# Cross-attention in a one-core decoder step: the samples' values weighed in column quarters of TensorE, all eight samples' values resident

## What is computed

```python
def cross_attend(h, w_xq, w_xo, mem_k, mem_v):
    b, l, _ = h.shape
    q = (h @ w_xq).reshape(b, l, X_HEADS, X_HEAD_DIM)
    s = jnp.einsum('blhd,bmhd->bhlm', q, mem_k).astype(F32) * (X_HEAD_DIM ** -0.5)
    p = jax.nn.softmax(s, axis=-1).astype(mem_v.dtype)
    o = jnp.einsum('bhlm,bmhd->blhd', p, mem_v).reshape(b, l, D_MODEL)
    return o @ w_xo
```

## Time and profile before

| | us |
|---|---|
| median of 3 runs (2934.2 to 2935.93) | 2935.62 |
| the profiled execution's own time | 2925.83 |
| span of the profiled execution | 2924.1 |
| phase `cross`, its first DMA issue to the first matmul of the next phase | 1924.57 to 2044.81 |

### The profile page before, as it was taken

One profiled execution on the slowest core, in us unless ns is written; L12 is line 12 of the kernel. 1 busy time (PEld: TensorE's weight loads), 2 busy tenths in 40 slices (PEclk: granted clock), 3 DMA queues, 4 the chain that ended last, 5 costly groups with the idle time before them and its releaser, 6 DMA issues. The chain is left out here.

```text
span 2924.1 us, 44166 instructions
## 1 busy us (share of the span) xinstructions
PE 2717.6 (93%) x15387; PEld 2195.3 (75%) x15387; DVE 1838.5 (63%) x2530; ACT 803.8 (27%) x1460; POOL 352.3 (12%) x581
## 2 busy tenths in 40 slices
PE   6789899999999999988879789988989999999998
PEld 4457666666666667865525789973989999999998
DVE  6559999899898937867552462564264444444445
ACT  4231211211111213049712541331051111111115
POOL 1010032322322211200122000031000000000000
PEclk7789999999999999999979799998999999999999
DMA  9876699989999835521197431144111111111111
GB/s 354 298 258 202 190 336 320 341 296 315 330 317 317 310 98 176 165 63 30 58 289 250 153 122 36 37 146 160 55 42 46 43 50 43 50 43 43 43 57 60
DMA packets 334116, 478.19 MB, mean 164 GB/s; under 512 B 26600, under 2 KB 215397, under 8 KB 332110
## 3 DMA queue, kind: packets, MB, share of 16 engines
q1 hardware_dynamic: 291110, 333.29, 34.5%
q0 software_dynamic: 42416, 142.32, 14.2%
q10 hardware_dynamic: 408, 0.31, 0.0%
HBM read 453.22 MB, written 22.62 MB: 163 GB/s over the span
## 5 line engine op out<-in xcount | busy, mean ns | idle before, releaser
L84 ACT ACTIVATE whi<-raw 128x1024 fp32r<-128x1024 f32 (+1 forms) x184 | 189.7, 1044 | 924.3 <-PE banks L113 807.7
L111 PE MATMUL banks<-ffn_hhi,whi 128*128 128x344 f32 x1056 | 339.9, 322 | 8.0 <-DVE ffn_hlo L141 5.1
L112 PE MATMUL banks<-ffn_hlo,whi 128*128 128x344 f32 x1056 | 338.6, 321 | 0.0
L113 PE MATMUL banks<-ffn_hhi,wlo 128*128 128x344 f32 x1056 | 338.6, 321 | 0.0
L111 PE MATMUL banks<-ffn_ghi,whi 128*128 128x344 f32 (+1 forms) x880 | 315.7, 359 | 10.8 <-DVE xT L1771 5.3
L113 PE MATMUL banks<-ffn_ghi,wlo 128*128 128x344 f32 (+1 forms) x880 | 310.8, 353 | 0.0
L112 PE MATMUL banks<-ffn_glo,whi 128*128 128x344 f32 (+1 forms) x880 | 309.8, 352 | 0.0
L88 DVE TENSOR_TENSOR wlo<-raw,whi 128x1024 fp32r<-128x1024 f32 (+1 forms) x184 | 222.5, 1215 | 134.7 <-ACT whi L84 134.4
L111 PE MATMUL banks<-a_hhi,whi 128*128 128x512 f32 x704 | 287.9, 409 | 6.9 <-DVE wlo L88 6.1
L624 DVE TENSOR_TENSOR ffn_kt<-ffn_kt,ffn_q 128x1024 f32<-128x1024 f32 x224 | 272.9, 1219 | 28.2 <-DMA ffn_kt<-in_cache_k_dram 28.2
L611 POOL DMA_DIRECT2D ffn_vt<-in_cache_v_dram x384 | 206.7, 538 | 654.4 <-issue 648.7
(11 more groups left out here) (474 smaller groups left out, 4762.8 us busy)
## 6 DMA issues: line engine op xcount, KB each, us to landing
ffn_kt<-in_cache_k_dram SPq DMA_DIRECT2D x448, 256.0 KB, 4.3
ffn_vt<-in_cache_v_dram POOLq DMA_DIRECT2D x384, 256.0 KB, 5.0
raw<-in_w_ffn_gate_dram SPq DMA_DIRECT2D x44, 512.0 KB, 4.5
raw<-in_w_ffn_up_dram SPq DMA_DIRECT2D x44, 512.0 KB, 4.1
raw<-in_w_ffn_down_dram SPq DMA_DIRECT2D x44, 512.0 KB, 4.6
last_kt<-in_cache_k_dram POOLq DMA_DIRECT2D x64, 256.0 KB, 3.1
s_vt<-in_cache_v_dram POOLq DMA_DIRECT2D x64, 256.0 KB, 5.1
s_vt<-in_cache_v_dram SPq DMA_DIRECT2D x64, 256.0 KB, 4.8
```

What stands on the lines that cost most here:

```text
L84: act.activation(self.k.whi[c % W_RING][:, 0:self.width], self.slots[s][:, 0:self.width], ACT.Copy).then_inc(self.hi_done, 1)
L111: pe.matmul(out, whi, rhi, start=first, stop=False)
L112: pe.matmul(out, whi, rlo, start=False, stop=False)
L113: return pe.matmul(out, wlo, rhi, start=False, stop=last)
```

## The change

In `cross`, the samples' values get eight places of their own: four in the space of `qT`, one in that of `mkT`, one in that of `qb`, and slots 2 and 3 of `cache`. SP loads them in three steps: five once the last scores are out (`sc_ps` at 8), one once the last product is done, two once the last keys are reduced. The next phase's first two weight blocks follow at once. PE takes four samples at a time: the matmul of sample `first + c` writes partitions 32c to 32c+31 of the bank, and the four matmuls of one k and half stand one behind the other. So each quarter of the 128 partitions holds the sum over two samples. `masked`, `mask` and `sel` grow from 32 to 128 partitions; the mask is made a quarter at a time, and POOL starts with its products only after that.

```diff
-        sel = place("c_sel", [32, NS], 44.9)
-        masked = place("c_masked", [32, D], 32.5)
-        mask = place("c_mask", [32, D], 137.5)
+        sel = place("c_sel", [P, NS], 44.9)
+        masked = place("c_masked", [P, D], 32.5)
+        mask = place("c_mask", [P, D], 137.5)
         qb = place("c_qb", [P, 2, D], 129.5)
         cache = place("c_cache", [P, 4, 2, D], 0, ring=True)
+        in_qT = place("c_v_in_q", [P, 4, 2, D], 97)
+        values = [in_qT[:, j] for j in range(4)] + [place("c_v_in_k", [P, 2, D], 48)[:, :, :], place("c_v_in_qb", [P, 2, D], 129.5)[:, :, :],
+                                                    cache[:, 2], cache[:, 3]]
...
                 def load(n):
                     if n >= 4:
-                        if n - 4 < NS:
-                            sp.wait_ge(q["reduced"], n - 3)
-                        else:
-                            sp.wait_ge(q["v_used"], n - 4 - NS + 1)
-                    src = a["cache_mem_k" if n < NS else "cache_mem_v"][n % NS].rearrange("(b p) n -> p b n", p=P)
-                    sp.dma_start(cache[:, n % 4], src).then_inc(cache_in[n % 4], 16)
+                        sp.wait_ge(q["reduced"], n - 3)
+                    sp.dma_start(cache[:, n % 4], a["cache_mem_k"][n].rearrange("(b p) n -> p b n", p=P)).then_inc(cache_in[n % 4], 16)
...
-                for n in range(2 * NS - 4):
-                    if n + 2 < NS:
-                        query(n + 2)
-                    load(n + 4)
+                for n in range(NS - 2):
+                    query(n + 2)
+                    if n + 4 < NS:
+                        load(n + 4)
+                sp.wait_ge(q["sc_ps"], GR)
+                for b in range(5):
+                    load_v(b)
+                sp.wait_ge(q["product"], NS)
+                load_v(5)
+                sp.wait_ge(q["reduced"], NS)
+                load_v(6)
+                load_v(7)
                 for n in range(RAW_RING):
-                    sp.wait_ge(q["v_used"], 5)
                     self.load_ahead(sp, "xo", n)
...
-                v.tensor_tensor(masked[:, :], self.psum[0:32, 1024:2048], mask[:, :], ALU.mult).then_inc(q["kept"], 1)
+                v.tensor_tensor(masked[:, :], self.psum[:, 1024:2048], mask[:, :], ALU.mult).then_inc(q["kept"], 1)
...
                 pe.wait_ge(q["exped"], GR)
-                for b in range(NS):
-                    pe.wait_ge(q["padded"], b + 1)
-                    pe.wait_ge(cache_in[b % 4], 16 * (2 + b // 4 + 1))
+                for first in (0, 4):
+                    pe.wait_ge(q["padded"], first + 4)
+                    for c in range(4):
+                        pe.wait_ge(v_in[first + c], 16)
                     for k in range(2):
                         for half in range(2):
-                            ins = pe.matmul(ps[2 + half][0:32, :], pad[:, b, k], cache[:, b % 4, k, half * 512:(half + 1) * 512],
-                                            start=b == 0 and k == 0, stop=b == NS - 1 and k == 1)
-                    ins.then_inc(q["all_v"] if b == NS - 1 else q["v_used"], 1)
+                            for c in range(4):
+                                b = first + c
+                                ins = pe.matmul(ps[2 + half][32 * c:32 * c + 32, :], pad[:, b, k], values[b][:, k, half * 512:(half + 1) * 512],
+                                                start=first == 0 and k == 0, stop=first == 4 and k == 1)
+                ins.then_inc(q["all_v"], 1)
```

More of the change, by code:

```diff
@@ L2994, in cross @@
         qb_in = [self.sem(f"c_qb_in{r}") for r in range(2)]
+        v_in = [self.sem(f"c_v_in{b}") for b in range(NS)]
         REDUCED_IN = {2: (0,), 3: (1,), 4: (2,), 5: (3, 4), 6: (5,), 7: (6, 7)}
@@ L3000, in load, with load_v @@
                     if n >= 4:
-                        if n - 4 < NS:
-                            sp.wait_ge(q["reduced"], n - 3)
-                        else:
-                            sp.wait_ge(q["v_used"], n - 4 - NS + 1)
-                    src = a["cache_mem_k" if n < NS else "cache_mem_v"][n % NS].rearrange("(b p) n -> p b n", p=P)
-                    sp.dma_start(cache[:, n % 4], src).then_inc(cache_in[n % 4], 16)
+                        sp.wait_ge(q["reduced"], n - 3)
+                    sp.dma_start(cache[:, n % 4], a["cache_mem_k"][n].rearrange("(b p) n -> p b n", p=P)).then_inc(cache_in[n % 4], 16)
+                def load_v(b):
+                    sp.dma_start(values[b], a["cache_mem_v"][b].rearrange("(b p) n -> p b n", p=P)).then_inc(v_in[b], 16)
                 def query(n):
@@ L3033, in _ @@
                 pool.wait_ge(q["consts"], 2)
[L3035 to L3040, removed]
+                for c in range(4):
+                    m3 = mask[32 * c:32 * c + 32, :].rearrange("p (h x) -> p h x", h=HEADS)
+                    pool.wait_ge(q["consts"], 2 + 2 * c)
+                    pool.affine_select(out=m3, in_=m3, compare_op=ALU.is_ge, fill=0.0, base=0, pattern=[[-8, HEADS], [0, NM]],
+                                       channel_multiplier=1).then_inc(q["consts"], 1)
+                    pool.wait_ge(q["consts"], 3 + 2 * c)
+                    pool.affine_select(out=m3, in_=m3, compare_op=ALU.is_ge, fill=0.0, base=7, pattern=[[8, HEADS], [0, NM]],
+                                       channel_multiplier=-1).then_inc(q["consts"], 1)
+                pool.wait_ge(q["consts"], 10)
                 for b in range(NS):
@@ L3081, in _ @@
             def _(v):
-                v.tensor_reduce(sel[:, :], self.ident[0:32, 0:32].rearrange("p (h b) -> p b h", b=NS), AX.X, ALU.add).then_inc(q["kept"], 1)
+                v.tensor_reduce(sel[:, :], self.ident[:, :].rearrange("p (h b) -> p b h", b=NS), AX.X, ALU.add).then_inc(q["kept"], 1)
                 for i in range(GR + 2):
@@ L3110, in _ @@
                         v.wait_ge(q["s_turned"], 2)
-                        v.wait_ge(q["consts"], 4)
+                        v.wait_ge(q["consts"], 10)
                         for b in range(NS):
```

2 lines of the change are left out of this document (1 added, 1 removed).

## The result

| | before | after |
|---|---|---|
| median, us (lowest to highest, runs) | 2928.69 (2918.93 to 2935.93, 7) | 2906.66 (2897.61 to 2912.31, 7) |
| ratio, 95% interval | | 0.9916 [0.9893, 0.994] |
| own time of the profiled execution | 2925.83 | 2897.61 |
| its span | 2924.1 | 2895.9 |
| phase `cross` in it, to the next phase's first matmul | 1924.57 to 2044.81 = 120.2 | 1918.49 to 2017.81 = 99.3 |

The change is faster by 22.0 us in the medians, or 0.84%. By the ratio it is 24.6 us, with an interval from 17.6 to 31.3. Four more runs of the kernel before came with the result, and they moved its median from 2935.62 to 2928.69.

A forecast was written before the change was run, and what follows sets the result against it. PE bounds the kernel, busy 93% of the span, with the samples' block in cross hiding nothing. Terms: -20.57 + 0.7 = -19.9 us; from a median of 2935.62 that gives 2915.7 us, range 2909.5 to 2923.5.

The forecast's parts named there:

- the last of the sum: Total time: the predicted difference set against the runs' median instead of the profiled 2925.83: 2935.62 - 19.9 = 2915.7 us.
- part 3: POOL's six extra mask selects in cross delay the first product, carried fully to the end: +0.7 us, bounds 0 to 2.3.
- Part 1: PE's block of samples' values matmuls in cross: quarters overlap, 27.65 to 7.08 us, a gain of 20.57 us.
- Rivals B to F: Half clock 2919-2923 (0.10); late loads 2920.8-2925.9 (0.05); slower packs 2917.3 (0.05); no overlap 2936.3 (0.03); array drains 2953.6 us (0.02).
- rival D: PE's block in cross: packs start staggered and load weights between, 8.7 instead of 7.08 us, total 2917.3; chance 0.05.
- Part 2: The samples' eight value loads in cross land before PE needs them: cost 0, with 5.8 us margin for the last.
- Part 4: Rest of cross: mask multiply on 128 partitions 0, gather contracting 128 rows at most 0.1 us, sel 0, tail unchanged.
- the clock: PE clock steps may shift: -1.9 to +1.9 us at the next phase's start, up to +7.1 if the block runs at half.

The follow-up runs named there:

- e8: The kernel before, run again unchanged under another name; ratio 1.0 [0.9981, 1.0018].
- e1: The changed kernel, run again unchanged beside the kernel before; median 2908.83 against 2933.47 us, ratio 0.9921 [0.9894, 0.9949].
- e4: Changed kernel's packing in quarters, but values in the old ring of four slots, second four loaded after the first pack; ratio to the kernel before 0.9958.
- e6: Changed kernel with every mask select issued twice, 16 on POOL ahead of the products; ratio to the kernel before 0.9922 [0.9894, 0.9949].
- e5: Changed kernel with POOL's mask selects moved behind the products; ratio to the kernel before 0.9932 [0.9908, 0.9957].
- e11: Changed kernel with mask selects behind the products and POOL's first product waiting for DVE's round 1 negation; ratio to the kernel before 0.9914 [0.9885, 0.9943].
- e9: Kernel before, plus a wait of POOL's first product for DVE's round 1 negation; median 2926.21 against 2932.44 us, ratio 0.9986.
- e10: Kernel before with the changed kernel's eight mask selects on POOL, nothing else; median 2933.04 against 2932.44 us, ratio 0.9997.
- e3: Changed kernel with the loop over samples moved outside, so each sample's four matmuls stand together in its quarter; ratio to the kernel before 0.9951.
- e7: Changed kernel with mask selects behind the products and the samples' block ahead of the prompt's last weighed values; ratio to the kernel before 0.992.

## Why the prediction was wrong

**The direction and the main mechanism were right; the time was not.** Forecast was -19.9 us; the medians moved by -22.0, and the ratio says -24.6 with an interval that holds 19.9. The time, 2906.66, lies 9.0 us below the forecast and 2.8 us below the range. Of the 9.0 us, 6.9 are the median of the kernel before (2935.62, then 2928.69) and 2.1 the difference.

**The step that failed is the last of the sum**, "its difference set against the median of the runs, which is 9.8 us higher: 2935.62 - 19.9". I took three runs within 1.7 us as the kernel's level, and gave the range no term for how executions differ. With the later runs the medians of before were 2928.69, 2933.47, 2932.29 and 2932.44, and single runs reached from 2918.93 to 2945.61. The warning stood in the prediction itself: a profiled execution 9.8 us below the median says that executions differ by as much. The same difference against 2928.69 would have given 2908.8, 2.1 us above the result, and even that lies 0.7 us below the range's end.

Neither set of seven runs is the last word. All 92 executions of the kernel before (the ten of e8 among them) have a median of 2932.6, all 16 of the changed kernel 2907.7, a difference of 24.9 us. By these the level was 3 us too high and the difference some 5 us too small, which points to a second fault in the sum; part 3 has a candidate.

**Where executions differ.** The 14 traces run the same code up to the phase, and it starts anywhere from 1917.5 to 1932.0; behind the phase they agree within 3.6 us (876.0 to 879.6). One large piece is the run of 64 matmuls of L1547 shown above, which begins between 83.5 and 86.5 us: it takes 5.9 us at a granted clock of 1.00 in six traces and 11.2 us at 0.50 in the other eight. With the 32 matmuls behind it that makes 7.8 us against 14.0 to 14.7. The six are just those whose phase starts earliest (1917.5 to 1922.4; the eight start at 1923.1 or later). What makes the clock fall in one execution and not in another was not tried.

**Part 1, the block: right to 0.01 us.** 7.08 was worked out, 7.07 measured in all six traces in which the interleaved block found its values on chip and the clock at full. Rivals B to F fell: full clock, no gap, no drain. The block ran 3.9 times as fast as before. The estimate behind rival D, from the 2.38 times for three column tiles in the Trainium skill (TensorE: Matmul & The Clock Gate, "Measured speedup vs the span model"), was 3.2 times, or 8.7 us. The drain that the Trainium skill (TensorEngine Tiling (Array Packing), "Key Properties") gives for a change of mode does not show at a change of quarter; where the block begins, behind matmuls on the full array, the step is 0.52 us instead of 0.43.

**Part 2, the loads: right.** Eight loads in one queue, and PE waited for none. The margin for the last was 5.1 us, where 5.8 had been forecast, and in e1 3.0. e4 shows what the places were for: without them PE waits 12.8 us.

**Part 3, the selects: the first step right, the rest not.** One collision, the first product at 11.6 us: forecast was +0.7, measured +0.87. "So I carry the 0.7 us through fully" then failed: in both traces the block came earlier in the phase (84.4 and 83.7) than in either trace of the kernel before (85.5 and 90.4), and in e6 a product 10.0 us later moved it by 6.7 to 7.4. Over all traces a first product between 10.75 and 11.62 gives a block at 82.4 to 85.5 in the old order of PE (9 traces); e5 and e8, at 9.85 and 10.07, have 91.8 and 90.4. What decides is whether the product begins ahead of DVE's negation at 10.6. Before the change that hung on when the first query landed; with the eight selects in front the product starts at 11.57 to 11.62 in all six traces. e11 against e5, and e9 against e8, show this race, each in single traces. It may be part of why the ratio's centre lies 4 us beyond the block's 20.6: the two traces of the kernel before have phases of 120.2 and 125.1 us, the two of the changed one 99.3 and 97.9, 24.1 apart in the mean. But that it moves the median was not shown: the interval holds 20.6, e10 moved no median, and how often plain runs of the kernel before start the product early is open.

**Part 4 and the clock.** The mask multiply (1.22 us, before 1.21) and the gather cost nothing more at equal clock: the gather takes 1.95 us in e1, as before, and 2.70 in the first trace, where the clock fell to half within it. The next phase's start lay in a half-clock stretch again, within the bounds given.

## What to carry to other kernels

Small matmuls gain in full from column quarters only if neighbours in the queue go to different quarters, and only if their operands are there: here grouping by quarter kept 11.8 us of the block's gain, packing without residency 5, residency without packing nothing, both 20.6. A wait that seems to be paid may order two engines that share something: before moving work out of the time ahead of it, look at what the other engine does in the microsecond behind. Ahead of writing down an absolute time, compare the profiled execution with the runs; if they are 10 us apart, so may the next median be.

## What the runs showed of the hardware

- Four fp32 matmuls of 32 columns each in four column quarters run at once, with four different moving operands: 64 records in 7.07 us against 27.65.
- Matmul records do not all start in program order. In e3 a matmul for a free quarter starts ahead of earlier ones that still wait for theirs, but only two quarters come to work at once (15.85 us for the 64 records).
- A DVE operation on four elements per partition, 0.17 us when free, takes 3.78 to 4.00 us when a POOL product of 4.5 us has just begun (e5, e7, e8). The Trainium skill (SBUF — State Buffer, "Terms") says that the port pair which GpSimd and VectorE share is held for the full instruction; e8's rows, where DVE is done when the product is, and e9's, where it starts first, agree.
- The same 64 matmul records took 5.9 us in six executions and 11.2 in eight, at granted clocks of 1.00 and 0.50.
